# Sliding attention on 144 keys per step instead of 256: one mask instruction per step, and zeros written by GpSimd

## The reference

```
bucket = t5_bucket(pq[..., :, None] - pk[..., None, :])
bias = rel_bias[bucket]...
qi = jnp.arange(BLOCK)[:, None] + BLOCK
kj = jnp.arange(2 * BLOCK)[None, :]
local = (kj <= qi) & (qi - kj < WINDOW)
first = (jnp.arange(nb)[:, None, None] > 0) | (kj[None] >= BLOCK)
s = jnp.einsum('bnqhgd,bnshd->bnhgqs', q, kb)
s = jnp.where(local & first, s * scale + bias, NEG)
m = jnp.maximum(jnp.max(s, axis=-1, keepdims=True), sink)
p = jnp.exp(s - m)
p = p / (jnp.sum(p, axis=-1, keepdims=True) + jnp.exp(sink - m))
o = jnp.einsum('bnhgqs,bnshd->bnqhgd', p, vb)
```

## Time and profile before

| | us |
|---|---|
| median of 3 runs | 3357.43 |
| lowest and highest of them | 3349.66, 3379.94 |
| the profiled execution | 3371.25 |
| span of the profiled execution, first to last instruction | 3370.1 |

### The profile page before, as it was taken

One profiled execution on the slowest core, in us unless ns is written; L12 is line 12 of the kernel. 1 busy time (PEld: TensorE's weight loads), 2 busy tenths in 40 slices (PEclk: granted clock), 3 DMA queues, 4 the chain that ended last, 5 costly groups with the idle time before them and its releaser, 6 DMA issues.

```text
span 3370.1 us, 31960 instructions
## 1 busy us (share of the span) xinstructions
PE 2931.8 (87%) x12180; PEld 1420.5 (42%) x12180; DVE 1176.9 (35%) x2966; ACT 630.7 (19%) x1531; POOL 284.5 (8%) x323
## 2 busy tenths in 40 slices
PE   4995999998985989999849999899998589999982
PEld 2543864444452333333324444455564533333330
DVE  5006964244444111111233000777723512121114
ACT  2102640000020111111013000565512111010001
POOL 0000000000001110110020000222400000101002
PEclk9996999999896999999979999999989599999996
DMA  7203003432515879889863010000100469898986
GB/s 260 100 0 100 20 14 101 136 100 97 202 52 224 335 305 379 317 358 363 349 225 130 25 50 0 22 19 25 38 2 19 178 232 394 350 400 349 395 347 229
DMA packets 177820, 610.30 MB, mean 181 GB/s; under 512 B 60418, under 2 KB 102914, under 8 KB 152964
## 3 DMA queue, kind: packets, MB, share of 16 engines
q1 hardware_dynamic: 112500, 531.35, 40.2%
q0 software_dynamic: 65168, 76.91, 6.9%
HBM read 557.27 MB, written 50.60 MB: 180 GB/s over the span
## 4 chain that ended last, share of the span: by engine, by line
PE 76%; DMA 11%; DVE 9%; issue 2%; ACT 1%; SPq 1%; POOL 0%; DVEq 0%; POOLq 0%; ACTq 0%
PE ps L1623 16%; DMA R<-in_w_up 8%; PE ps L1599 7%; PE ps L919 7%; PE ps L2139 6%; PE ps L1025 3%; PE ps L2571 3%; PE ps L437 3%; PE ps L2136 3%; PE ps L923 3%; PE ps L734 2%; PE ps L443 2%; PE ps L1574 2%; PE ps L2380 2%; PE ps L1583 1%
## 5 line engine op out<-in xcount | busy, mean ns | idle before, releaser
L1623 PE MATMUL ps<-R 128*64 128x512 f32 x1520 | 725.2, 622 | 79.7 <-DMA R<-in_w_up 73.0
L1624 PE MATMUL ps<-R 128*64 128x512 f32 x1520 | 725.6, 623 | 0.0
L1623 PEld LDWEIGHTS ps<-R 128*64 128x64 f32 x1520 | 207.2, 143 | 495.7 <-issue 483.5
L1599 PE MATMUL ps<-R 128*64 128x512 f32 x1520 | 342.4, 592 | 2.1 <-DVE R L1471 2.1
L919 PE MATMUL ps<-R 128*128 128x512 f32 x512 | 230.5, 609 | 0.5 <-ACT R L713 0.5
L2139 PE MATMUL ps<-R 128*128 128x512 f32 x512 | 220.5, 592 | 1.6 <-DVE R L1961 1.6
L1624 PEld LDWEIGHTS ps<-R 128*64 128x64 f32 x1520 | 207.1, 143 | 0.0
L1599 PEld LDWEIGHTS ps<-R 128*64 128x64 f32 x1520 | 108.6, 137 | 217.5 <-issue 214.9
L1497 DVE TENSOR_TENSOR R<-ps,R 64x512 f32<-64x512 f32 x95 | 64.8, 683 | 344.4 <-ACT R L1542 195.5
L1471 DVE COPY R<-ps 128x256 f32<-128x256 f32 x95 | 40.3, 425 | 410.8 <-PE ps L1583 410.8
L1529 ACT ACTIVATE R<-ps,small 128x128 f32<-128x128 f32 (+1 forms) x200 | 74.1, 451 | 574.5 <-PE ps L1574 574.5
(11 more groups left out here) (322 smaller groups left out, 3763.9 us busy)
## 6 DMA issues: line engine op xcount, KB each, us to landing
R<-in_w_gate SPq DMA_DIRECT2D x64, 2048.0 KB, 13.7
R<-in_w_up SPq DMA_DIRECT2D x64, 2048.0 KB, 14.1
R<-in_w_down SPq DMA_DIRECT2D x64, 2048.0 KB, 19.5
R<-in_w_ada SPq DMA_DIRECT2D x40, 1024.0 KB, 5.4
R<-in_w_in SPq DMA_DIRECT2D x13, 2048.0 KB, 8.5
YE<-R POOLq DMA_DIRECT2D x48, 256.0 KB, 24.0
YE<-acc POOLq DMA_DIRECT2D x34, 256.0 KB, 18.9
R<-in_w_ada SPq DMA_DIRECT2D x4, 2048.0 KB, 15.6
```

The source lines that it names most:

```text
L1599: i_ = T.matmul(k.ps[64 * hf:64 * hf + 64, 5 + b % 2, :], v.hT[b % 2][:, kk, :], v.down[n % RING][:, kk, 512 * hf:512 * hf + 512], start=k ...
L1623: T.matmul(k.ps[64:128, b % 2, :], x_, wg[:, kk, :], start=kk == 0, stop=kk == 7)
L1624: i_ = T.matmul(k.ps[0:64, b % 2, :], x_, wu[:, kk, :], start=kk == 0, stop=kk == 7)
```

## The change

`window_of` now returns three things: from step 8 on the first key is `128 * (qb - 1) + 16 * sub` and the number of keys is 144; the third value, `at = 16 * sub`, is where these keys lie within the 256 columns of `SS`. `tiles_of` gives the key tiles for transposes and values, which stay at two of 128. The score matmuls, the masks, the maximum, the exponential and the normalising are done on 144 columns; the transposes, their copy and the value matmuls still take 256.

The four masks of a step are written by one `tensor_tensor` over 4 x `nk` elements with both operands broadcast. The columns of `SS` that a step no longer writes must be zero: the new function `gpsimd_attn` writes zeros there (256 columns for steps 8 to 10, then 48 or 80), after the transposes of three steps earlier, and DVE now waits for that (`g_clr`) instead of for the transposes.

```
 def window_of(T0):
-    qb = T0 // 8
-    return (128 * (qb - 1), 256) if qb else (0, 128)
+    qb, sub = T0 // 8, T0 % 8
+    return (128 * (qb - 1) + 16 * sub, 144, 16 * sub) if qb else (0, 128, 0)
+def tiles_of(T0):
+    return (T0 // 8 - 1, 2) if T0 // 8 else (0, 1)
+def gpsimd_attn(k):
+    G, s = k.nc.gpsimd, k.s
+    v = attn_views(k)
+    for T0 in range(8, 64):
+        sub = T0 % 8
+        if T0 < 11:
+            c0, c1 = 0, 256
+        elif sub >= 3:
+            c0, c1 = 16 * sub - 48, 16 * sub
+        else:
+            c0, c1 = 16 * sub + 144, 16 * sub + 224
+        G.wait_ge(s["p_pt"].sem, T0 - 2)
+        G.memset(v.SS[T0 % 3][:, c0:c1], 0.0).then_inc(*s["g_clr"].up())
...
     def masks(T0):
...
-        for j in range(4):
-            V.tensor_scalar(v.stp[T0 % 2][j][:, 0:nk], v.posf[:, k0:k0 + nk], v.PQ[:, T0 * 4 + j:T0 * 4 + j + 1],
-                            None, ALU.is_le).then_inc(*mk.up())
+        V.tensor_tensor(v.stp[T0 % 2][:, :, 0:nk], v.posf[:, k0:k0 + nk].unsqueeze(1).broadcast_to([128, 4, nk]),
+                        v.PQ[:, 4 * T0:4 * T0 + 4].unsqueeze(2).broadcast_to([128, 4, nk]),
+                        ALU.is_le).then_inc(*mk.up())
...
-            w0 = (112 - 16 * sub) + (0 if qb else 128)
+            w0 = 112 if qb else 240 - 16 * sub
...
-            if T0 >= 3:
+            if T0 >= 8:
+                V.wait_ge(s["g_clr"].sem, T0 - 7)
+            elif T0 >= 3:
                 V.wait_ge(s["p_pt"].sem, T0 - 2)
-            V.tensor_tensor_reduce(v.SS[T0 % 3][:, 0:nk], k.ps[:, T0 % 3, 0:nk], ...
+            V.tensor_tensor_reduce(v.SS[T0 % 3][:, at:at + nk], k.ps[:, T0 % 3, 0:nk], ...
...
-            V.tensor_scalar(v.SS[X % 3][:, 0:nk], v.SS[X % 3][:, 0:nk], es, None, ALU.mult)
+            V.tensor_scalar(v.SS[X % 3][:, at:at + nk], v.SS[X % 3][:, at:at + nk], es, None, ALU.mult)
...
-            S.activation(v.SS[T0 % 3][:, 0:nk], v.SS[T0 % 3][:, 0:nk], ACT.Exp, bias=nm,
+            S.activation(v.SS[T0 % 3][:, at:at + nk], v.SS[T0 % 3][:, at:at + nk], ACT.Exp, bias=nm,
                          accum_out=dn).then_inc(*ex.up())
...
+            T.wait_ge(s["v_mask"].sem, T0 + 1)
             for j in range(4):
-                T.wait_ge(s["v_mask"].sem, 4 * T0 + j + 1)
                 for s3 in range(3):
...
     gpsimd_zero_rows(k)
+    gpsimd_attn(k)
     n = gpsimd_experts(k, 0)
```

More of the change, by code:

```diff
@@ L97 @@
     "v_ln a_ln p_ws v_ws p_sv "
-    "v_prep v_mask v_max v_nrm a_exp a_pt a_ya p_sc p_pt p_ov "
+    "v_prep v_mask g_clr v_max v_nrm a_exp a_pt a_ya p_sc p_pt p_ov "
     "p_mg a_sig v_mg p_mod v_fin "
@@ L596, in attn_views @@
     v.wfull = v.wf.rearrange("p (q h) -> p q h", h=8)
-    v.stp = [[k.acc[:, 512 * u + 128 * j:512 * u + 128 * j + 128].bitcast(BF16) for j in range(4)] for u in range(2)]
+    v.stp = [k.acc[:, 512 * u:512 * u + 512].bitcast(BF16).rearrange("p (j t) -> p j t", j=4) for u in range(2)]
     v.PT = [TMP[:, 2848 + 256 * u:3104 + 256 * u] for u in range(2)]
@@ L650, in masks @@
     def masks(T0):
-        k0, nk = window_of(T0)
+        k0, nk, _ = window_of(T0)
         if T0 >= 2:
             V.wait_ge(s["p_sc"].sem, T0 - 1)
-        for j in range(4):
-            V.tensor_scalar(v.stp[T0 % 2][j][:, 0:nk], v.posf[:, k0:k0 + nk], v.PQ[:, T0 * 4 + j:T0 * 4 + j + 1],
-                            None, ALU.is_le).then_inc(*mk.up())
+        V.tensor_tensor(v.stp[T0 % 2][:, :, 0:nk], v.posf[:, k0:k0 + nk].unsqueeze(1).broadcast_to([128, 4, nk]),
+                        v.PQ[:, 4 * T0:4 * T0 + 4].unsqueeze(2).broadcast_to([128, 4, nk]),
+                        ALU.is_le).then_inc(*mk.up())
     V.wait_ge(s["d_zero"].sem, 32)
@@ L664, in vector_attn @@
             qb, sub = T0 // 8, T0 % 8
-            _, nk = window_of(T0)
-            w0 = (112 - 16 * sub) + (0 if qb else 128)
+            _, nk, at = window_of(T0)
+            w0 = 112 if qb else 240 - 16 * sub
             mx, nm, _, _ = (k.sm[T0 % 2][:, c:c + 1] for c in range(4))
             V.wait_ge(s["p_sc"].sem, T0 + 1)
-            if T0 >= 3:
+            if T0 >= 8:
+                V.wait_ge(s["g_clr"].sem, T0 - 7)
+            elif T0 >= 3:
                 V.wait_ge(s["p_pt"].sem, T0 - 2)
-            V.tensor_tensor_reduce(v.SS[T0 % 3][:, 0:nk], k.ps[:, T0 % 3, 0:nk], k.C("win")[:, w0:w0 + nk], 1.0, NEG,
+            V.tensor_tensor_reduce(v.SS[T0 % 3][:, at:at + nk], k.ps[:, T0 % 3, 0:nk], k.C("win")[:, w0:w0 + nk], 1.0, NEG,
                                    ALU.add, ALU.max, mx).then_inc(*mxs.up())
@@ L676, in vector_attn @@
             X = T0 - 1
-            _, nk = window_of(X)
+            _, nk, at = window_of(X)
             dn, es = (k.sm[X % 2][:, c:c + 1] for c in (2, 3))
@@ L683, in vector_attn @@
             V.wait_ge(nrm.sem, nrm.n)
-            V.tensor_scalar(v.SS[X % 3][:, 0:nk], v.SS[X % 3][:, 0:nk], es, None, ALU.mult).then_inc(*nrm.up())
+            V.tensor_scalar(v.SS[X % 3][:, at:at + nk], v.SS[X % 3][:, at:at + nk], es, None, ALU.mult).then_inc(*nrm.up())
 def scalar_attn(k):
@@ L702, in scalar_attn @@
             X = T0 - 2
-            _, nk = window_of(X)
+            nk = 128 * tiles_of(X)[1]
             S.wait_ge(s["p_pt"].sem, X + 1)
@@ L730, in tensor_attn @@
                      start=True, stop=False)
+            T.wait_ge(s["v_mask"].sem, T0 + 1)
             for j in range(4):
-                T.wait_ge(s["v_mask"].sem, 4 * T0 + j + 1)
                 for s3 in range(3):
-                    i_ = T.matmul(o, k.wb3[:, s3, 128 * j:128 * j + 128], v.stp[T0 % 2][j][:, 0:nk],
+                    i_ = T.matmul(o, k.wb3[:, s3, 128 * j:128 * j + 128], v.stp[T0 % 2][:, j, 0:nk],
                                   start=False, stop=(j == 3 and s3 == 2))
@@ L742, in tensor_attn @@
                 T.wait_ge(s["a_pt"].sem, X - 1)
-            for c in range(nk // 128):
+            for c in range(tiles_of(X)[1]):
                 i_ = T.transpose(k.ps[:, 3 + X % 2, 128 * c:128 * c + 128], v.SS[X % 3][:, 128 * c:128 * c + 128],
@@ L748, in tensor_attn @@
             X = T0 - 3
-            _, nk = window_of(X)
-            k0b = X // 8 - 1 if X // 8 else 0
+            k0b, n2 = tiles_of(X)
             T.wait_ge(s["a_pt"].sem, X + 1)
@@ L753, in tensor_attn @@
                 T.wait_ge(s["a_ya"].sem, X - 1)
-            n2 = nk // 128
             for c in range(n2):
```

## The result

| | kernel before | changed kernel |
|---|---|---|
| median (runs) | 3368.68 us (4) | 3321.64 us (4) |
| lowest and highest | 3349.66, 3386.11 | 3319.66, 3333.43 |
| span of the profiled execution | 3370.1 us | 3332.2 us |

The ratio is 0.9876, with a 95% interval of 0.983 to 0.9921: 0.8 to 1.7% less, which is clear of no change, though the interval reaches over the 1% at which the prediction drew its line. The forecast was 3320.7 us and 36.7 us less; the medians differ by 47.0 us, since the kernel before is now at 3368.68 and not at 3357.43. The two traces differ by 37.9 us of span. Between the first mask and the first matmul of the merge lie 154.0 us before (319.47 to 473.47) and 116.6 us after: 37.4 us less.

The account below looks back on a forecast made before the run. TensorE's 2.41 us attention step bounds the kernel before, VectorE's 2.31 close behind. 56 steps at 1.75 us save 36.0 us; with 0.9 + 0.2 - 0.4, 36.7 off 3357.43 gives 3320.7 us, range 3307 to 3346.

Parts of the forecast that it names:

- VectorE's queue: VectorE's (DVE's) own work in one attention step of the changed kernel: 1.75 us, taken as the limit that sets the step.
- the loop through ScalarE: Maximum, exponential, copy of PT, values, scores, maximum two steps later: 3.39 us for two steps, 1.70 a step.
- The sum: Attention's 56 steps from the maximum of step 7: 97.9 us for 133.92; with the ends, 36.7 us less.
- The mask instruction: One tensor_tensor of 576 elements on VectorE: 0.757 us, 0.672 from start to start; bounds 0.4 and 1.1 us.
- The bias matmuls: Twelve matmuls a step on TensorE at 144 columns: 0.062 us apart, 0.75 us in place of 1.31.
- the 81 ns: Skill's matmul spacing at 128 columns; by it twelve bias matmuls take 1.0 us, TensorE's step 1.9, stage gain about 27.
- From the last maximum to the merge: End of the attention stage: one narrower maximum, exponential and normalising in its chain, 0.2 us less.
- the slower side: Rival: TensorE's clock falls to 1.2 GHz in the new stage, step 3.32 us, 52 us more, 3409; chance 0.04.
- The beginning: First eight attention steps, 128 keys: step 1.83 to 1.66 us; first three gain nothing, five gain 0.9 us.
- The sign that I named: Expected in the changed trace: step 1.75 us, PE's gap ended by the normalising, no gap on DVE.
- The memsets: GpSimd's 56 zero writes: 0.15 us each, under the masks, ending over 1 us ahead of the maximum, costing nothing.
- The rest: Everything after the attention, from the merge on, was to move up rigidly by the stage's gain.

Follow-up runs that it names:

- experiment 1: Also `k144_four`: the changed kernel with the four separate mask instructions back, 144 keys each; steady step 1.886 us, against 1.74 in the changed kernel.
- experiment 3: The kernel before with score and bias matmuls on 144 columns from step 8 on, everything else on 256; steady step 2.294 us.
- experiment 4: The changed kernel with two of the four masks left out from step 8 on; steady step 1.745 us, two steps 3.49 us.
- experiment 6: The changed kernel with two of four masks left out from step 8 on and ScalarE's copy of PT ahead of its exponential; steady step 1.663 us.
- Experiment 7: The changed kernel without GpSimd's zeros from step 11 on, VectorE waiting for the transposes again; step 1.744 us.
- experiment 9: Also `late_memset`: the changed kernel with a second GpSimd memset of 700 columns in each step, waiting for the negated maximum; steady step 1.969 us.
- after_again: The changed kernel again, in a second comparison with its own runs of both kernels; median 3327.80 us, ratio to the kernel before 0.9891.
- long_memset: The changed kernel with a second GpSimd memset of 700 columns in each step, right behind the first; steady step 1.746 us.
- k256_one: The kernel before with one mask instruction in place of four, still 256 keys; steady step 2.409 us, as before.
- add_early: The changed kernel with ScalarE's copy ahead of its exponential and the sum of exponentials on GpSimd; median 3318.49 us, ratio to the kernel before 0.9868.

## Why the prediction was right

**The limit that it named is not quite the one that ends last.** The prediction put VectorE's queue at 1.75 us and the loop through ScalarE at 1.70. They are 1.738 and 1.745: the queue is right to 0.01 us, the loop was 0.05 too short, and so the two have changed places. The forecast of the step held because they lie 7 ns apart, and this is luck. What the mechanism had right is that narrowing TensorE's work is worth nothing without VectorE's part (experiments 1 and 3).

**The sum held, term by term.** From maximum to maximum I had 97.9 us for 56 steps and it was 97.6. The mask instruction was to take 0.757 us and took 0.751; from its start to the next 0.672, measured 0.67. The bias matmuls were to be 0.062 us apart: twelve took 0.75 us in the chain, as forecast; the 81 ns that the Trainium skill gives for 128 columns ("TensorE: Matmul & The Clock Gate", section "Back-to-back issue gap") are not what this trace shows, at 144 columns either. From the last maximum to the merge it was 4.59 us for 4.80, 0.2 less as forecast.

**The clock** was 1.00 from 328 us on in the changed kernel, so the slower side had nothing.

**The beginning was slightly mis-sized.** From the first maximum to that of step 7 the trace has 12.14 us after and 13.43 before (321.32 to 334.75): 1.3 us less, where I had 0.9. Half of the 0.4 us lies in the second interval, 2.04 us for 2.22: I had let the first three steps gain nothing because PE was busy at half clock. The other half lies in the last, 1.71 for 2.10, in which VectorE writes the masks of step 8: they were already 256 keys wide before, and I had costed this interval like the others. The later start of the first bias matmul (0.4 us) was as forecast: from the first mask to the first maximum 1.85 us before, 2.26 after (318.51 to 320.77).

**The loop through ScalarE was mis-sized: 3.39 us forecast, 3.49 measured**. The missing 0.10 us lies between the weights of the values and the end of the scores: 388.45 to 390.16 is 1.71 us in experiment 4, my terms gave 0.45 + 0.24 + 0.75 + 0.17 = 1.61. It is in the values: from their first weight load to the query-key matmul it is 0.55 us there (388.45 to 389.00), where the chain of experiment 6, with no wait, has 0.45. A float32 weight load starts 0.1 us ahead of its matmul (388.90 and 389.00 for the query-key matmul). In an unbroken row the matmul before it covers this time; behind a wait nothing does, and I had counted the matmuls as an unbroken row. This reading fits the 0.10 us, but no run changes the load alone. The consequence is small in the sum, large in the picture: not one limit at 1.75 and another at 1.70, but two at 1.74.

**The sign that I named was wrong.** "PE's gap ended by the normalising" does not occur. PE's only wait is the one for ScalarE's copy. It shows neither in the busy time nor in the chain, only as 0.06 us between two weight loads, too short for a view to mark it; the normalising ended at 386.34, 0.3 us before the transposes started. Had I trusted the chain, which is all PE, I would have found my own theory refuted; experiment 1 shows the same chain in a kernel whose step follows the masks.

**The memsets** cost nothing, but not for the reason given. I placed them under the masks; they start with the end of the transposes, which PE does later than I had it, and so lie over the end of the maximum. They ended 1.37 us ahead of the maximum that needs the zeros (385.56 to 386.93), over 1 us as forecast. Experiment 7 shows that they are free, experiment 9 what a memset costs that meets the normalising: 0.22 us a step.

**The rest moved up, though not rigidly.** These are the first instructions of the merge (above and 473.47 before), the second block's projections, and the last line:

```profile
L2160 PE MATMUL ps<-R x512: 592/592/1173, 1740.7 to 2020.3; 128*128 128x512 f32 x171
```
```profile
L1927 DVE SCALAR_TENSOR_TENSOR XR<-XR,small,R x8: 1279/1280/1285, 3309.7 to 3327.9; 128x1024 f32<-128x1024 f32 x8
```

The merge was 38.3 us earlier, the second block's projections (L2139 before, from 1772.7) 32.0 us, the last line (L1906 before, from 3347.6) 37.9 us. Some 6 us were lost between the merge and the second block's projections (1299.2 us before, 1305.6 after) and came back later. That is scatter and not the change: the same changed kernel took 1294.9 us for this stretch in `after_again`. From the merge to the end of the span it is 2896.6 us before, 2897.1 after, and in other kernels whose work from there on is the same 2892.8 (`after_again`), 2877.8 (`long_memset`) and 2888.5 (`k256_one`). These 19 us of spread are half of the gain. That the median came out within 1 us of the forecast is partly luck, as the differences of 47.0 and 26.2 us around the forecast 36.7 show; that the stage became 37.4 us shorter is not luck in its size, though it is in the order of the two limits.

## What to carry to other kernels

When two engines are within a few per cent of each other, cost both parts of a change together: narrow matmuls alone gave 0.12 us of 2.41, one mask instruction alone nothing, 144 keys on both engines 0.52 (experiment 1), and with the one mask instruction 0.67 (0.664 from the steady steps). A step that is 100% PE in the chain and in the busy share can still be set by another engine; look for an operation whose share of the chain is longer than its plain cost, look at how long before an instruction its inputs were ready, and change one engine's work to see whether the step follows. Then take the second limit away as well: a step that does not follow may be held by another limit. After a gain of this kind look for the next limit at once: here it was already 7 ns away, in a written order of ScalarE that can be turned with nothing left out (turning it alone gave 7 ns a step).

## What the runs showed of the hardware

- A `tensor_scalar` from SBUF to SBUF that meets a GpSimd memset ends 0.09 us after the memset does (`long_memset`, `late_memset`): it took 0.34 to 0.37 us where the memset ended 0.25 to 0.29 us after its start, 0.59 where it ended 0.50 us after it, and 0.295 alone. A memset of 48 columns took 0.21 us in place of 0.14 where it started during a `tensor_scalar` (`k144_four`).
- One `tensor_tensor` over four short rows with both operands broadcast and bfloat16 output (576 elements, 0.751 us) costs no more than the line through the rows of 512 and 1,024 elements of the kernel before gives for that length (0.757).
- A one-column `tensor_tensor` took 0.31 us on GpSimd in `add_early` and 0.15 on VectorE.
